# Mixer output tile by tile, tile 0's first expert head routed ahead of tile 1's last product, and the other expert queries placed inside the gather stream

## What is computed

```python
mix = (g[:, :, 0] * attn + g[:, :, 1] * pool + g[:, :, 2] * conv) @ w_out    # g = sigmoid of a projection
h = h + mod[:, 2] * mix
xn2 = modulate(rms_norm(h, norm2_g[l]), mod[:, 3], mod[:, 4])
h = h + mod[:, 5] * peer_ffn(xn2, peer_wq[l], peer_keys[l], peer_u[l], peer_v[l])
```

## Time and profile before

| | |
|---|---|
| median of 3 runs | 3764.11 (3760.03 to 3773.43) |
| profiled execution, its own time | 3767.54 |
| its span | 3766.2 |
| mean granted TensorE clock | 0.927 |
| busy, share of the span | PE 82%, DVE 52%, POOL 41%, ACT 10% |
| DMA | 1125.52 MB, mean 299 GB/s |

### The profile page before, as it was taken

How to read it: one execution, slowest core, us unless ns; L and a number is a source line. 1 busy time by engine, 2 the same in 40 slices (tenths; PEclk the granted TensorE clock), 3 DMA queues, 4 the chain that set the end, 5 groups by cost and what they waited for, 6 DMA issues and landing times.

```text
span 3766.2 us, 30999 instructions
## 1 busy us (share of the span) xinstructions
PE 3080.4 (82%) x11474; PEld 1345.9 (36%) x11474; DVE 1977.0 (52%) x4448; ACT 366.5 (10%) x923; POOL 1527.7 (41%) x1579
## 2 busy tenths in 40 slices
PE   7999887789989888688888889887567667798897
PEld 4484445234523326222222224546111111144343
DVE  0051447787756625766666523356777776213132
ACT  1000320120000001000000000231000000002111
POOL 0010003666656652666666631003677777500000
PEclk9999998899999989899999989999898998899999
DMA  6274137999999997999999987317999999941322
GB/s 271 96 292 170 78 123 293 368 358 404 409 397 406 388 363 288 379 411 411 411 411 412 411 322 291 131 68 299 375 409 409 407 407 398 357 154 72 113 90 100
DMA packets 257376, 1125.52 MB, mean 299 GB/s; under 512 B 29636, under 2 KB 34980, under 8 KB 238024
## 3 DMA queue, kind: packets, MB, share of 16 engines
q0 software_dynamic: 221184, 805.40, 54.4%
q1 hardware_dynamic: 32456, 312.82, 21.3%
q10 hardware_dynamic: 3584, 5.31, 0.4%
HBM read 1117.06 MB, written 6.37 MB: 298 GB/s over the span
## 4 chain that ended last, share of the span: by engine, by line
PE 42%; DMA 25%; DVE 18%; POOL 8%; issue 4%; ACT 2%; DVEq 0%; SPq 0%; ACTq 0%
DMA big<-in_u,xT 17%; PE ps L234 16%; POOL big L2137 7%; DMA big<-in_v,xT 7%; DVE big L2106 6%; PE ps L1966 5%; PE ps L1905 5%; PE ps L656 4%; PE ps L1399 2%; PE ps L670 1%; PE ps L1435 1%; DVE small L910 1%; PE ps L387 1%; PE ps L587 1%; PE ps L248 1%
## 5 line engine op out<-in xcount | busy, mean ns | idle before, releaser
L1966 PE MATMUL ps<-big,bc 128*32 128x512 f32 x3072 | 1069.8, 666 | 341.2 <-DMA big<-in_v,xT 328.7
L2106 DVE CUSTOM_DVE_ANT_0 big<-big,ps 128x1024 f32<-128x1024 f32 x768 | 926.2, 1215 | 415.3 <-DMA big<-in_u,xT 411.4
L2137 POOL DMA_INDIRECT big<-in_u,xT x768 | 727.5, 947 | 589.6 <-issue 165.4
L2137 POOL DMA_INDIRECT big<-in_v,xT x768 | 729.5, 950 | 277.9 <-issue 187.2
L234 PE MATMUL ps<-w,xT 128*128 128x512 f32 x1408 | 619.5, 601 | 8.6 <-ACT xT L256 5.7
L1966 PEld LDWEIGHTS ps<-big,bc 128*32 128x32 f32 x3072 | 193.6, 115 | 1101.8 <-DMA big<-in_v,xT 736.8
L234 PEld LDWEIGHTS ps<-w,xT 128*128 128x128 f32 x1408 | 269.9, 193 | 349.6 <-issue 336.9
L524 POOL TENSOR_TENSOR small<-small 128x32 f32<-128x32 f32 (+1 forms) x8 | 33.2, 4154 | 374.5 <-DVE small L495 249.8
L1905 PE MATMUL ps<-tmp,w 128*128 128x256 f32 x768 | 170.6, 384 | 2.0 <-ACT tmp L256 2.0
L656 PE MATMUL ps<-w,xT 128*128 128x512 f32 x384 | 167.1, 594 | 1.7 <-ACT bb L755 0.9
L1905 PEld LDWEIGHTS ps<-tmp,w 128*128 128x128 f32 x768 | 147.4, 193 | 23.5 <-ACT tmp L256 3.2
(11 more groups left out here) (305 smaller groups left out, 2772.8 us busy)
## 6 DMA issues: line engine op xcount, KB each, us to landing
w<-in_w_in SPq DMA_DIRECT2D x58, 2048.0 KB, 9.2
bc<-in_w_mod SPq DMA_DIRECT2D x21, 2048.0 KB, 10.7
w<-in_w_conv SPq DMA_DIRECT2D x24, 1536.0 KB, 9.1
w<-in_peer_wq SPq DMA_DIRECT2D x12, 2048.0 KB, 9.2
w<-in_w_out SPq DMA_DIRECT2D x10, 2048.0 KB, 8.1
w<-in_conv_out_w SPq DMA_DIRECT2D x6, 2048.0 KB, 8.5
big<-in_u,xT POOLq DMA_INDIRECT x768, 10.6
big<-in_v,xT POOLq DMA_INDIRECT x768, 11.0
```

The lines of the kernel that those rows point to most:

```text
L1966: ins = pe.e.matmul(self.ps[32 * g:32 * g + 32, 2 + half, :], p["diag"][part % 2][:, 256 * g + 32 * m:256 * g + 32 * m + 32], p["ring"][:, ...
L2106: dve.inc(dve.e.tensor_tensor_reduce(out=row, in0=row, in1=p["xc"], scale=1.0, scalar=0.0, op0=ALU.mult, op1=ALU.add, accum_out=p["hid"][t ...
L2137: ins = pool.e.indirect_dma_start(p["ring"][:, slot, :], None, table, bass.IndirectOffsetOnAxis(index, 0))
```

## The change

- **Mixer output by tile.** PE makes the gates as tile 0 chunk 0, tile 0 chunk 1, tile 1 chunk 0, transposes of tile 0, tile 1 chunk 1. Then come `w_out` products of tile 0 chunk 0, transposes of tile 1, tile 0 chunk 1, tile 1 chunk 0, and (layer 1) the line bias. The merged tiles are turned into a place in `big`, and tile 0's gates use another part of `tmp` and no longer wait for DVE's norm of the attention.
- **Tile 0's first head first.** Calls 1 and 3 begin with tile 0 alone: its norm, transposes, queries 0 and 1 in 128 columns from a 1 MB copy of their weights loaded early (`first_w`), scores of head 0, and only then tile 1's chunk 1 product, queries 2 and 3 of tile 0, scores of head 1. DVE routes head 0 ahead of tile 1's last residual and norm, whose power POOL computes after four gathers. Tile 1's transposes follow, and its first four queries.
- **Queries inside the stream.** The others (16 in calls 1 and 3, 10 in call 2) go into the program at places `int(k * 1.6)` of the `u` places, on PE and on ACT, so the last is at place 24 and 14. Side work starts at place 27 (call 1) and 18 (call 2).
- **Loads.** The norm's rows go into `bb` and `bc`, the keys are loaded before `w_out`, and the line bias's tables and rows now stand on SP's queue behind call 3's first query load.

```diff
+QUERY_PACE = 1.6
...
+    def expert_rows(self):
+        return self.bb[:, 2 * D:3 * D], self.bc[:, 5, :], self.bb[:, 3 * D:4 * D]
+
+    def expert_rows_sp(self, sp, l, name):
+        rows = (self.d["norm2_g"][l:l + 1, :], self.mod_row(l, 0, 3)(1), self.mod_row(l, 0, 3)(0))
+        for n, (row, dst) in enumerate(zip(rows, self.expert_rows())):
+            self.load_row(sp, 3 + n, row, name, n, dst=dst)
...
+    def expert_norm_act(self, act, l, tile):
+        act.wait_ge(self.dve, f"mix{l}", "added", tile)
+        act.inc(act.x.activation(self.merged[:, tile, :], self.h[:, tile, :], ACT.Square, accum_out=self.small[:, 8 + tile:9 + tile]), f"norm2{l}0", "squares", tile)
...
 
         self.gated_sp(sp, l, 0, None)
+        self.first_q_in.inc(sp.e.dma_start(self.first_w(), self.columns("peer_wq", l, 0)[:, :, 0:2 * P]), "first wq", l)
         self.after(sp, ("att", l))
         self.mods_stored(sp, l, range(2, 6))
         self.load_row(sp, 0, self.mod_row(l, 0)(2), "gate2", l, 0)
-        self.norm_sp(sp, f"norm2{l}0", (3, 4, 5), self.d["norm2_g"][l:l + 1, :], self.mod_row(l, 0, 3))
+        self.expert_rows_sp(sp, l, f"norm2{l}0")
+        self.keys_in.inc(sp.e.dma_start(self.peer_views()["keys"], self.d["keysT"][l]), f"peer{l}0", "keys")
         self.residual_sp(sp, f"mix{l}", "w_out", l, 1)
+
+    def first_w(self):
+        return self.big[:, 2, 0:2 * D].rearrange("p (k n) -> p k n", k=KC)
+
+    def mixT(self):
+        return self.big[:, 1, 2 * D:4 * D].rearrange("p (k t) -> p k t", k=KC)
...
+    def mix_turn_pe(self, pe, l, tile):
+        pe.wait_ge(self.dve, ("gated", l, 0), "merge", 1, tile)
+        for half in range(2):
+            for j in range(4):
+                k = 4 * half + j
+                ins = pe.e.transpose(self.ps[:, 4 + 2 * tile + half, j * P:(j + 1) * P], self.merged[:, tile, k * P:(k + 1) * P], self.ident[:, :])
+            pe.inc(ins, f"mT{l}", "turn", 2 * tile + half)
+
+    def mix_product_pe(self, pe, l, tile, c):
+        pe.wait_ge(self.w_in[c], "w", f"mix{l}", c)
+        pe.wait_ge(self.act, ("gated", l, 0), "tanh", c, tile)
+        pe.wait_ge(self.act, f"mT{l}", "turned", 2 * tile + 1)
+        for k in range(KC):
+            ins = pe.e.matmul(self.ps[:, 2 * tile + c, :], self.mixT()[:, k, tile * P:(tile + 1) * P], self.wk(c)[:, k, :],
+                              start=k == 0, stop=k == KC - 1)
+        pe.inc(ins, f"mix{l}", "mm", c, tile)
+
+    def mix_pe(self, pe, l):
+        name = ("gated", l, 0)
         self.after(pe, ("att", l))
-        self.gated_pe(pe, l, 0, tiles, None)
-        self.end(pe, f"attended{l}")
-        self.after(pe, f"attended{l}")
-        self.transposed_pe(pe, f"mT{l}", lambda t: self.merged[:, t, :], len(tiles))
-        pe.wait_ge(self.act, f"mT{l}", "turned", 2 * len(tiles) - 1)
-        self.linear_pe(pe, f"mix{l}", self.lhs, tiles, 2, self.dve, beside=lambda c: l and not c and self.bias_pe(pe))
-        self.end(pe, f"mixed{l}")
+        for tile in range(2):
+            for c in range(2):
+                pe.wait_ge(self.w_in[c], "w", name, "gate", c)
+                for k in range(KC):
+                    ins = pe.e.matmul(self.ps[:, 2 * tile + c, :], self.lhs(k, tile), self.wk(c)[:, k, :], start=k == 0, stop=k == KC - 1)
+                pe.inc(ins, name, "gate", c, tile)
+                if tile and not c:
+                    self.mix_turn_pe(pe, l, 0)
+        self.mix_product_pe(pe, l, 0, 0)
+        self.mix_turn_pe(pe, l, 1)
+        self.mix_product_pe(pe, l, 0, 1)
+        self.mix_product_pe(pe, l, 1, 0)
+        if l:
+            self.bias_pe(pe)
 
     def layer0_act(self, act):
         for n in range(2):
...
+    def mix_act(self, act, l):
         self.after(act, ("att", l))
-        act.wait_ge(self.dve, "att normed", l)
-        self.gated_act(act, l, 0, tiles, None)
-        self.end(act, f"attended{l}")
-        self.after(act, f"attended{l}")
-        self.transposed_act(act, f"mT{l}", len(tiles), self.xT)
-        self.expert_norm_act(act, f"norm2{l}0", f"mix{l}")
-        self.end(act, f"mixed{l}")
+        self.gate0_act(act, l, 0, 0)
+        self.gate0_act(act, l, 0, 1)
+        self.gate0_act(act, l, 1, 0)
+        self.mix_turned_act(act, l, 0)
+        self.gate0_act(act, l, 1, 1)
+        self.mix_turned_act(act, l, 1)
+        self.expert_norm_act(act, l, 0)
...
+    def mix_dve(self, dve, l):
         self.att_norm_dve(dve, l)
         dve.mark("att normed", l)
-        self.gated_dve(dve, l, 0, tiles, None, False)
-        self.end(dve, f"attended{l}")
+        self.mix_merge_dve(dve, l, 0)
...
+        self.mix_merge_dve(dve, l, 1)
+        self.mix_residual_dve(dve, l, 0, 0)
+        self.mix_residual_dve(dve, l, 0, 1)
+        self.expert_norm_dve(dve, f"norm2{l}0", 0)
+
+    def mix_last_dve(self, dve, l):
+        self.mix_residual_dve(dve, l, 1, 1)
+        self.expert_norm_dve(dve, f"norm2{l}0", 1)
...
-                               ("mix", 27, [dve] * 4)], 16, 500)
+                               ("mix", 27, [dve] * 4)], 27, 500)
...
+    def query_items(self, stream):
+
+        if stream:
+            return [(i, 0, 2) for i in range(16)]
+        return [(i, tile, tile + 1) for tile in range(2) for i in range(4)] + [(i, 0, 2) for i in range(4, 16)]
+
+    def query_order(self, stream):
+
+        first = 6 if stream else 4
+        n = len(self.query_items(stream))
+        return {e: [q for q in range(first, n) if int((q - first) * QUERY_PACE) == e] for e in range(PART)}
+
+    def last_query(self, stream, chosen, tile):
+        return max(n for n, (i, t0, t1) in enumerate(self.query_items(stream)) if i in chosen and t0 <= tile < t1)
...
+            last = self.last_query(stream, range(4 * c, 4 * c + 4), 1)
+            self.load_w(sp, c % 2, [(self.wk(c % 2), self.columns("peer_wq", l, c))], (name, "q", last), name, c)
+            if c == 0 and l:
+                self.bias_sp(sp)
             if c == 1:
                 sp.wait_ge(self.dve, f"norm2{l}{stream}", "normed")
-                self.keys_in.inc(sp.e.dma_start(keys, self.d["keysT"][l]), name, "keys")
+                if stream:
+                    self.keys_in.inc(sp.e.dma_start(keys, self.d["keysT"][l]), name, "keys")
                 self.load_row(sp, 0, row(5), name, "gate")
...
+        def query(n):
+            i, t0, t1 = items[n]
             c, g = i // 4, i % 4
-            if not g:
+            if stream or n > 1:
                 pe.wait_ge(self.w_in[c % 2], "w", name, c)
-            if i >= 3:
-                pe.wait_ge(self.act, name, "q out", i - 3)
+                w = self.wk(c % 2)
+            else:
+                pe.wait_ge(self.first_q_in, "first wq", l)
+                w = self.first_w()
+            if n >= 3:
+                pe.wait_ge(self.act, name, "q out", n - 3)
             for k in range(KC):
-                ins = pe.e.matmul(self.ps[:, 5 + i % 3, 0:256], self.wk(c % 2)[:, k, g * P:(g + 1) * P], p["xT"][:, k, :],
+                ins = pe.e.matmul(self.ps[:, 5 + n % 3, t0 * P:t1 * P], w[:, k, g * P:(g + 1) * P], p["xT"][:, k, t0 * P:t1 * P],
                                   start=k == 0, stop=k == KC - 1)
-            pe.inc(ins, name, "q", i)
+            pe.inc(ins, name, "q", n)
...
-            query(i)
+        if stream:
+            pe.wait_ge(self.dve, f"norm2{l}{stream}", "normed")
+            self.transposed_pe(pe, f"{name} xT", lambda t: self.merged[:, t, :], 2)
+            pe.wait_ge(self.act, f"{name} xT", "turned", 3)
+        else:
+            pe.wait_ge(self.dve, f"norm2{l}0", "normed", 0)
+            tokens_turned(0)
+        for n in range(2):
+            query(n)
         scores(0)
-        for i in range(2, 6):
-            query(i)
-        scores(1)
-        for i in range(6, 16):
-            query(i)
+        if stream:
+            for n in range(2, 6):
+                query(n)
+            scores(1)
+        else:
+            self.mix_product_pe(pe, l, 1, 1)
+            if l:
+                pe.wait_ge(self.dve, "line")
+            for n in range(2, 4):
+                query(n)
+            scores(1)
+            pe.wait_ge(self.dve, f"norm2{l}0", "normed", 1)
+            tokens_turned(1)
+        paced = self.query_order(stream)
         for at, (kind, e) in enumerate(self.peer_order()):
             yield at
             part, n = e // PART, e % PART
             if kind == "u":
+                for q in paced.get(e, ()):
+                    query(q)
                 step = e // TOPK
                 if e % TOPK == 0 and step % 2:
                     turn_experts(part)
...
+        else:
+            tokens_turned(0)
+            for n in range(2):
+                query(n)
+            self.gate_exp_act(act, name, p, 0)
+            for n in range(2, 4):
+                query(n)
+            self.expert_norm_act(act, l, 1)
+            tokens_turned(1)
+        paced = self.query_order(stream)
```

(39 more changed lines are left out.)

145 lines of the change are left out of this document (81 added, 64 removed).

## The result

The changed kernel takes **3744.35 us** (median of 6 runs, 3736.28 to 3750.64) against 3766.23 for the kernel before in the same runs: ratio 0.9938, 95% interval 0.9924 to 0.9952. The ratio says 0.62%, some 23 us (the medians themselves lie 21.9 apart), where 31 were forecast: clear of the noise, inside the range, 11 us short of the forecast of 3733, and within 1 us of rival (a)'s 3745. The profiled execution took 3748.13 us, 3746.8 of them its span (3766.2 before).

What follows compares the result with a forecast made beforehand. It took each expert call to be a stream of 512 gathers limited by the DMA engines. Gains of 18 (call 1), 5 (call 2) and 8 (call 3) made 31 us: 3733 us on the median, range 3718 to 3749.

Steps and rivals of the forecast that it cites:

- rival (a): Calls 1 and 2: TensorE as the bound; call 1 gives 11, call 2 nothing, call 3 8: 19 us, 3745; chance 0.22.
- Call 1's start: Layer 0 tokens: first gather 22.7 us earlier, first dot 20.5 earlier, from mixing by tile and the early first head.
- The exponential's stall: Call 1, DVE waiting for ACT's exponential: 3 us of stall where 8 were.
- Side work: Call 1: context stream starts at place 27, not 16; costs 0 to 8.8 us, taken as 2.5, so call 1 gives 18.
- Rival (d): Calls 1 and 2: late side weights, 39 loads on the path, 46 us, 3779 us, slower; chance 0.03.
- Call 2: Layer 0 context: third-head experts 9.7 us earlier, less 5 for a load pushed into the full stream: gains 5, ends 3 and 9.7.
- Call 3: Layer 1 tokens: the tables' wait gives 11.5 us back; first gather 10.9 earlier, first dot 8 earlier, gain 8.
- Tile 1's norm beside the gathers: Calls 1 and 3, norm on DVE beside the first gathers: costed at nothing, bound 3.9 us in each call.
- the range's upper end: Whole kernel: 3749 us, from rival (a) with 4 us less, a gain of 15.

Runs made afterwards that it cites:

- the experiment: Changed kernel with call 2 alone put back (queries ahead of place 0, side work from place 1): 3744.67 us, ratio to before 0.9942.
- the first and last groups: First: four single edits of the changed kernel (before: 3767.0 us); last: the changed kernel unedited (3745.11 us) and three edited versions (3722.68 to 3729.88 us).

## Why the prediction was right or wrong

*Call 1's start: right, and a little too small.* First gather 67.3 us after the gates (forecast 70.0), with eight transposes 1.04 where 1.6 stood and two queries 3.84 where 4.2 did. First dot 75.7 (forecast 78.7), so tile 1's norm ended 8.4 us after the first gather, as costed. The exponential's stall is 3.19 (forecast 3) and the cast 112.9 after the gates (forecast 116.3). The change gave 25.4 us there against 22.7.

*Side work: the term that failed.* "Eleven places are worth 8.8 us of PE work ... I take 2.5." Measured, call 1 is 18.5 us longer from its first gather. I priced the shift of the plan by the PE work in it and never asked at which place the projection changes its weight chunk: half its 34 places after the start, at 33 before and at 44 after. The load has no lead whatever, for it goes into the slot that PE is using. Two slots gave back 12.3 us by one pair of traces and 8.4 by the other. The remaining 6 to 10 us lie about the upper bound of my term. No run takes them apart, but the trace with two slots shows where they go: its stream is 6.0 us ahead of the kernel before at place 64 (114.6 after the first gather, against 120.6) and 9.4 behind at place 256. POOL's waits for PE's value sums over places 128 to 256, in the kernel before and then with two slots:

```profile
POOL big L2137 <- PE ps L1966: 29.0, 20, 6.0
```

```profile
POOL big L2286 <- PE ps L2075: 40.5, 25, 5.2
```

The DMA share over these places is 1.01 before and 0.99 with two slots. That is what denser side work on PE would look like; it isn't shown to be its cause. Rival (d) named late side weights, but as a thinner lead for 39 loads at 1 us each; it is one load without a lead, at 8 to 12, and "a load comes every 36 us" said nothing of the lead: the trace before had two such loads with waits of 10.5 and 8.1.

*Call 2: sign right, size off.* Of 9.7 us, 6.5 arrived at place 40, and 4.8 of them went by the end, as the 5 us for the load pushed out of the hole had it. The load went out 88.1 us after the first gather, at place 50 (53.8 before, so that it landed in the hole), and then, in the changed kernel:

```profile
1554.33 1.22 DVE L2251 CUSTOM_DVE_ANT_0 big<-big,ps 128x1024 f32<-128x1024 f32 x1 [5.56 <-DMA big<-in_u,xT]
...
1565.50 0.94 POOL L2286 DMA_INDIRECT big<-in_u,xT  x1 [4.76 <-DVE xT L2170]
```

DVE waits for a `u` gather, its routing is late by that, and POOL waits for the routing at place 66. That hole (4.5 to 5.4 us) is in all eight traces on such chips in which side work starts at place 18, the one without pacing among them, and in neither of the two in which it starts at 0 or 1. The term was 5, measured is 1.7 in the trace and 1 to 3 by the experiment. Call 2's preparation was also 2.5 us longer. Its first two queries, in the kernel before and in the changed one:

```profile
1437.12 7.17 PE L1905 MATMUL ps<-tmp,w 128*128 128x256 f32 x32 [0.68 <-ACT tmp L256]
```

```profile
1433.06 9.52 PE L1996 MATMUL ps<-tmp,w 128*128 128x256 f32 x32 [0.67 <-ACT tmp L259]
```

The granted clock there was 1.00 over 1437 to 1441 before and 0.50 over 1433 to 1437 after; the code is the same, and so it is in five other traces of the first and last groups, in which these queries took 7.17 as before, one of them the changed kernel unedited. So this comes and goes between executions and isn't the change's; the reason was not tested.

*Call 3: right by mechanism and close in size.* 11.5 us given back by the tables was the term; the first gather came 11.2 earlier (forecast 10.9), and taking the wait away gave 12.4. The call gained 10.4 (forecast 8). The tables landed 7.2 and 7.3 us after their issue, 8.1 after that of the 2 MB load ahead (8.4 in the earlier trace rows), and PE waited 8.18. The rule from the Trainium skill (DMA: Bandwidth & Descriptors, Anatomy of one DMA), by which the wait would be near 3 us, does not carry over: the page measured it for a single DMA issued by GpSimd, and these are issued by SP with a 2 MB load ahead. The Trainium skill (DMA: Bandwidth & Descriptors, Queues, rings and completion order) says that each DMA engine consumes a queue's descriptors in ring order, and with that these landings agree.

*Tile 1's norm beside the gathers.* One gather took 2.00 us (566.81) where most take 0.94; the next are normal. That is 1.1 us of the 3.9 in the bound. It is the fifth gather, in calls 1 and 3 alike and in every trace of the changed kernel, while DVE runs the norm's two products; gathers right after other operations of POOL took 1.01 to 1.15. The trap of the Trainium skill (SBUF — State Buffer, "DVE blocks DMA") may be that one gather, though the page names fp32 copies and these are products; no run takes them away. Place 16 is 1.4 us later in call 1 and not at all in call 3 (33.2 in both), so it decides nothing.

*The rivals.* The total is rival (a)'s, and the larger part of its cause is not. It gave call 1 11 us by a bound of TensorE, but with one load moved and no PE work removed the kernel takes 3732.6, what I had forecast, and 6.8% denser side work did not lengthen call 1 in either trace. For the 6 to 10 us that are left, (a) is neither shown nor excluded. I had written that I was wrong if the first dots came early and the calls' ends did not follow within 5 us: in call 1 that is what happened. That the total lies inside the range is in part luck, for the range's upper end was drawn for (a). A right total here would have hidden a wrong term; 18, 5 and 8 became 6.9, 1.7 and 10.4.

## What to carry to other kernels

When a plan of side work is shifted, list each place where it changes a weight buffer and ask what the stream does there; a load into the buffer in use has no lead, and is free only in a hole that is there anyway. The trace before the change lists such loads already, as waits of PE for weights. Put a matmul's small tables ahead of the large load on the same queue, so that they don't wait for its slot either, and price such a wait with the cold clock behind it, here half as much again. An earlier first step is worth only what the next serial step takes over: pacing was needed for it, and a still earlier cast showed no gain, since the gathers were not there.

## What was not expected of the hardware

PE's granted clock fell to 0.50 after one wait of 8.18 us and was there over the 8 us of the two windows shown. A 2 MB load in the full stream reached PE 11.0 us after its issue (658.52 to 669.52), little over the 9.2 of the middle; the cost was the missing lead, not a slow load. The same two queries at the start of call 2 took 7.17 us in some executions and some 9.5 in others with the same code; the granted clock was 1.00 in the former and 0.50 at the start of the latter. Two chips differed by 3% in the kernel before (3767 and 3881 us), and the later side plan alone cost 24 us on the slower one.
